# Earlier output products and cheaper pair products in a two-layer hybrid encoder

## The reference

```python
def even_mixer(...):            # S 256, 8 heads of 128, chunks along the sequence
    qkv = silu(centred_dwconv(p[..., :c1], conv_qkv))
    o = gated_delta_rule(q, k, v, g0, beta0) + flip(gated_delta_rule(flip(q), ...))
    o = o * rsqrt(mean(o * o, -1) + RMS_EPS) * out_gain
    y_dn = o * silu(gate)
    y_sc = b_gate * centred_dwconv(c_gate * u_in, conv_sc)
    return concatenate([y_dn, y_sc]) @ w_out          # 1024 + 1024 rows of w_out

def odd_mixer(...):             # RWKV: 8 heads of 64
    y = scan_forward + scan_backward
    yn = (y - mean(y)) * rsqrt(var(y) + RW_GN_EPS) * ln_w + ln_b   # per head
    y_d = (yn + bonus_0 + bonus_1) * gate
    return concatenate([y_c, y_d]) @ w_out            # y_c: attention, 512; y_d: 512
```

## Time and profile before

| | us |
|---|---|
| median of 3 runs | 3043.23 (3040.58 to 3050.79) |
| profiled execution, its own time | 3038.12 |
| its span, first to last instruction | 3036.0 |
| PE busy in the span | 2929.5 |
| even scan's four groups, from 378 | to 545 |
| first product of ev_out | 574.01 |
| odd scan's four groups, from 1896 | to 2126 |
| first product of od_out | 2143.79 |

### The profile page before, as it was taken

How to read it: one execution, slowest core, us unless ns; L and a number is a source line. 1 busy time by engine, 2 the same in 40 slices (tenths; PEclk the granted TensorE clock), 3 DMA queues, 4 the chain that set the end, 5 groups by cost and what they waited for, 6 DMA issues and landing times.

```text
span 3036.0 us, 45974 instructions
## 1 busy us (share of the span) xinstructions
PE 2929.5 (96%) x19074; PEld 2682.3 (88%) x19074; DVE 1569.0 (52%) x1923; ACT 1271.0 (42%) x1564; POOL 186.2 (6%) x169
## 2 busy tenths in 40 slices
PE   8999999899999999999999997999999999999999
PEld 7999989788998989899898896888888989898897
DVE  4555456565544454544545466543655444544544
ACT  4543322364544534444444444122455434444443
POOL 0000055100000000000000001432000000000000
PEclk9999999999999999999999999888999999999999
DMA  6454300344455555555445550001344555545554
GB/s 255 167 193 181 139 1 1 120 172 153 167 184 191 183 194 188 187 193 181 166 167 180 201 194 18 1 1 56 111 167 139 188 187 182 192 182 194 181 185 149
DMA packets 67918, 462.31 MB, mean 152 GB/s; under 512 B 7007, under 2 KB 10079, under 8 KB 12940
## 3 DMA queue, kind: packets, MB, share of 16 engines
q1 hardware_dynamic: 63680, 449.95, 41.6%
q10 hardware_dynamic: 3500, 5.21, 0.5%
q0 software_dynamic: 544, 4.19, 0.4%
HBM read 457.21 MB, written 5.27 MB: 152 GB/s over the span
## 4 chain that ended last, share of the span: by engine, by line
PE 90%; DVE 6%; ACT 2%; DMA 1%; issue 1%; POOL 0%; SPq 0%; DVEq 0%; ACTq 0%; POOLq 0%
PE bank L406 13%; PE bank L407 13%; PE bank L408 13%; PE bank L381 12%; PE bank L382 12%; PE bank L383 12%; PE bank L1028 3%; PE bank L1012 2%; PE bank L2008 1%; PE bank L1225 1%; PE bank L507 1%; DVE hT_lo L520 1%; DVE split_lo L332 0%; DMA par<-in_small 0%; DMA hwork<-bias_rows 0%
## 5 line engine op out<-in xcount | busy, mean ns | idle before, releaser
L332 DVE TENSOR_TENSOR split_lo<-raw,split_hi 128x1024 fp32r<-128x1024 f32 x840 | 1026.6, 1225 | 1089.8 <-ACT split_hi L325 1088.9
L325 ACT ACTIVATE split_hi<-raw 128x1024 fp32r<-128x1024 f32 x840 | 889.2, 1061 | 1289.3 <-PE bank L408 677.1
L406 PE MATMUL bank<-hT_hi,split_hi 128*128 128x256 f32 x3376 | 957.0, 283 | 10.3 <-issue 4.5
L407 PE MATMUL bank<-hT_lo,split_hi 128*128 128x256 f32 x3376 | 956.1, 283 | 0.0
L408 PE MATMUL bank<-hT_hi,split_lo 128*128 128x256 f32 x3376 | 956.0, 283 | 0.0
L406 PEld LDWEIGHTS bank<-hT_hi,split_hi 128*128 128x128 f32 x3376 | 648.7, 192 | 8.3 <-DVE split_lo L332 3.6
L407 PEld LDWEIGHTS bank<-hT_lo,split_hi 128*128 128x128 f32 x3376 | 648.7, 192 | 5.1 <-issue 4.8
L408 PEld LDWEIGHTS bank<-hT_hi,split_lo 128*128 128x128 f32 x3376 | 648.8, 192 | 0.0
L381 PE MATMUL bank<-split_hi,u_hi 128*128 128x512 f32 x1152 | 449.4, 390 | 0.0
L382 PE MATMUL bank<-split_lo,u_hi 128*128 128x512 f32 x1152 | 448.3, 389 | 0.0
L383 PE MATMUL bank<-split_hi,u_lo 128*128 128x512 f32 x1152 | 448.3, 389 | 0.0
(11 more groups left out here) (393 smaller groups left out, 2356.7 us busy)
## 6 DMA issues: line engine op xcount, KB each, us to landing
raw<-in_stream SPq DMA_DIRECT2D x420, 1024.0 KB, 4.8
work<-in_mem POOLq DMA_DIRECT2D x2, 2048.0 KB, 9.2
bias_rows<-bias_line SPq DMA_DIRECT2D x1, 3072.0 KB, 15.0
hwork<-bias_rows ACTq DMA_DIRECT2D x2, 1536.0 KB, 9.6
x<-in_x SPq DMA_DIRECT2D x1, 2048.0 KB, 9.4
out<-x SPq DMA_DIRECT2D x4, 512.0 KB, 5.0
const<-in_masks SPq DMA_DIRECT2D x1, 1665.5 KB, 12.9
work<-in_wide ACTq DMA_DIRECT2D x1, 1280.0 KB, 5.8
```

The source lines that it names most:

```text
L325: nc.scalar.activation(split_hi[:, u % SPLIT], raw[:, b % RAW, (u % 2) * UNIT:(u % 2 + 1) * UNIT], ACT.Copy).then_inc(s_hi, 1)
L332: nc.vector.tensor_tensor(split_lo[:, u % SPLIT], raw[:, b % RAW, (u % 2) * UNIT:(u % 2 + 1) * UNIT], f32(split_hi[:, u % SPLIT]), SUB).th ...
L406: nc.tensor.matmul(out, lhsT=w_hi[:, cols], rhs=hT_hi[:, k, :], start=k == 0, stop=False)
L407: nc.tensor.matmul(out, lhsT=w_hi[:, cols], rhs=hT_lo[:, k, :], start=False, stop=False)
```

## The change

Five edits; its lines stand up to 54 lower than the same ones before.

1. `ev_out` takes the convolution half first: its weight rows are stored in that order, k tiles 8 to 15 of hT are read before 0 to 7, hT of the convolution half is written earlier and in four pieces, and PE's 16 transpositions stand behind units 2 and 3 of chunk 0. The dummy products are gone. ACT and DVE split two more units before their waits for the transpositions.
2. The RWKV norm is by group: statistics of each group right behind its output copy; scaling of groups 0 to 2 in one pass, of group 3 in another. POOL prepares gate times ln_w, and (bonus + ln_b) times gate, in four passes of 128 x 1024 in groups 0 and 1. `od_out` starts with the attention half, and the transpositions of groups 2 and 3 stand behind its unit 1.
3. `pe_delta_pre` computes key and query products for direction 0 only; direction 1 reads them from banks 2 and 3.
4. The last group's output goes to bank 2 instead of 0 in both layers.
5. `pe_rwkv_pairs` goes by tile, then by matrix, with the two heads (row halves) innermost; groups 1 to 3 have four dummy products ahead of the wait of direction 0.

```diff
-            pe_keep_busy(bank[1], 11)
-            for b in range(4):
-                pe.wait_ge(s_y, b // 2 + 1)
...
-            pe_out_cross(pe, 0, "ev_out", KD, lambda k: pe.wait_ge(s_yT, min(k // 2 + 2, 5)))
+            def turn_heads(u):
+                if u not in (2, 3):
+                    return
+                pe.wait_ge(s_y, u - 1)
+                for b in range(2 * u - 4, 2 * u - 2):
...
+            pe_out_cross(pe, 0, "ev_out", KD, lambda k, t: hT_tile((k + 8) % KD, t),
+                         lambda k: pe.wait_ge(s_yT, k // 2 + 1), turn_heads)
...
+OUT_BANK = (0, 0, 0, 2)
-                    for bk, lhsT, rhs in ((b[0], g_col, const_of("causal", 2 * d + 1)), (b[1], b_col, ident),
-                                          (b[2], dn_kT[:, h, tile], dn_kT[:, h, tile]),
-                                          (b[3], dn_kT[:, h, tile], dn_qT[:, h, tile])):
+                    products = [(b[0], g_col, const_of("causal", 2 * d + 1)), (b[1], b_col, ident)]
+                    if d == 0:
+                        products += [(bank[2], dn_kT[:, h, tile], dn_kT[:, h, tile]),
+                                     (bank[3], dn_kT[:, h, tile], dn_qT[:, h, tile])]
...
             act_delta_tail(act, DN_GROUPS - 1, range(3))
+            act.wait_ge(s_qtg, 2 * DN_GROUPS)
+            for b in range(4):
+                nc.scalar.activation(hT_hi[:, 8 + 2 * b:10 + 2 * b, :], yscT[:, 2 * b:2 * b + 2, :], ACT.Copy).then_inc(s_ysp, 1)
             act.wait_ge(s_oms, 1)
             nc.scalar.activation(o_sd, o_ms, ACT.Sqrt).then_inc(s_osd, 1)
+            hi_upto(act, starts["ev_out"][1] + AHEAD + 2)
...
             dve_delta_R(dve, DN_GROUPS - 1)
+            for b in range(4):
+                dve.wait_ge(s_ysp, b + 1)
+                nc.vector.tensor_tensor(hT_lo[:, 8 + 2 * b:10 + 2 * b, :], yscT[:, 2 * b:2 * b + 2, :],
+                                        f32(hT_hi[:, 8 + 2 * b:10 + 2 * b, :]), SUB).then_inc(s_yT, 1)
             dve_delta_out(dve, DN_GROUPS - 1)
...
-            pe_keep_busy(bank[3], 30)
-            pe.wait_ge(s_ry, 1)
...
+            turn_heads(0)
+            pe_out_cross(pe, 1, "od_out", 8, hT_tile, lambda k: pe.wait_ge(s_yT, 9 + k // 2),
+                         lambda u: turn_heads(1) if u == 1 else None)
...
+            if f and d == 0:
+                pe_keep_busy(bank[3], 4)
...
-            for i in range(2):
-                for t in range(NT):
-                    bk = pair_banks(f, d)[2 * i + t]
-                    rows = slice(64 * i, 64 * i + 64)
-                    for j, lhs in enumerate((btl[f % 2], ktl[f % 2])):
+            for t in range(NT):
+                for j, lhs in enumerate((btl[f % 2], ktl[f % 2])):
+                    for i in range(2):
+                        bk = pair_banks(f, d)[2 * i + t]
+                        rows = slice(64 * i, 64 * i + 64)
...
             dve_rwkv_state(dve, RW_F - 1)
+            dve_rwkv_norm(dve, 0, 3, 2)
+            for b in range(2):
+                dve.wait_ge(s_ysp, b + 9)
...
             dve_rwkv_out(dve, RW_F - 1)
-            dve.wait_ge(s_os, RW_F + 4)
...
+            dve_rwkv_norm(dve, 3, 1, 3)
...
+            dve.wait_ge(s_os, f + 5)
+            y = y_heads(Ytok, f, 1)
+            dve_step(nc.vector.reduce_sum(norm_of(gsum, f, 1), y, AX_X))
+            dve_step(nc.vector.tensor_scalar(norm_of(gmean, f, 1), norm_of(gsum, f, 1), 1.0 / RW_N, None, MULT))
+            dve_step(nc.vector.tensor_tensor(y, y, wide_of(gmean, f, 1), SUB))
+            dve_step(nc.vector.tensor_tensor(y_heads(y_sq, 0, 1), y, y, MULT))
+            dve_step(nc.vector.reduce_sum(norm_of(gvar, f, 1), y_heads(y_sq, 0, 1), AX_X))
+            nc.vector.tensor_scalar(norm_of(gms, f, 1), norm_of(gvar, f, 1), 1.0 / RW_N, GN_EPS, MULT, ADD).then_inc(s_oms, 1)
...
+        def dve_rwkv_norm(dve, f, n, root):
+            dve.wait_ge(s_osd, root)
+            dve.wait_ge(s_gnw, 1)
+            y, own = y_heads(Ytok, f, n), slice(f * P, (f + n) * P)
+            dve_step(nc.vector.reciprocal(norm_of(grs, f, n), norm_of(gsd, f, n)))
+            dve_step(nc.vector.tensor_tensor(y, y, wide_of(grs, f, n), MULT))
+            dve_step(nc.vector.tensor_tensor(Ytok[:, :, own], Ytok[:, :, own], gout[:, :, own], MULT))
+            nc.vector.tensor_tensor(Ytok[:, :, own], Ytok[:, :, own], y_add[:, :, own], ADD).then_inc(s_y, 1)
...
+                    if f < 2 and level in (2, 3):
+                        pool_norm_weights(pool, 2 * f + level - 2)
```

More of the change, by code:

```diff
@@ L275, in build @@
             sem(n) for n in ("s_rc", "s_rF", "s_rRA", "s_rbk", "s_rM", "s_rMAT", "s_rbt", "s_rBK", "s_rz1", "s_rz1s"))
-        s_gms, s_gsd, s_ry, s_ryt = (sem(n) for n in ("s_gms", "s_gsd", "s_ry", "s_ryt"))
+        s_gnw = sem("s_gnw")
         block = ctx.enter_context(nc.Block())
@@ L1265, in pe_delta_tail @@
                     for i in range(2):
-                        out = bank[0][:, (2 * t + i) * P:(2 * t + i + 1) * P]
+                        out = bank[OUT_BANK[hp]][:, (2 * t + i) * P:(2 * t + i + 1) * P]
                         qkt = QKT[hp % 2]
@@ L1501, in dve_even @@
                 nc.vector.tensor_tensor(y_tok[:, :, own, :], y_tok[:, :, own, :], g4, MULT).then_inc(s_y, 1)
-            dve.wait_ge(s_ysp, 1)
-            nc.vector.tensor_tensor(hT_lo[:, 8:16, :], yscT, f32(hT_hi[:, 8:16, :]), SUB).then_inc(s_yT, 1)
+            lo_upto(dve, starts["ev_out"][1] + AHEAD + 2)
             for b in range(4):
-                dve.wait_ge(s_ysp, b + 2)
+                dve.wait_ge(s_ysp, b + 5)
                 nc.vector.tensor_tensor(hT_lo[:, 2 * b:2 * b + 2, :], aux[b][:, :].rearrange("p (h s) -> p h s", s=S),
@@ L1964, in pe_rwkv, with turn_heads @@
                 pe_rwkv_tail(pe, RW_F - 1, step)
-            pe_keep_busy(bank[3], 30)
-            pe.wait_ge(s_ry, 1)
-            for b in range(2):
+            def turn_heads(b):
+                pe.wait_ge(s_y, b + 3)
                 for i in range(2):
@@ L2066, in pe_rwkv_tail @@
                             h = 2 * f + i
-                            out = bank[0][:, t * P + i * RW_N:t * P + (i + 1) * RW_N]
+                            out = bank[OUT_BANK[f]][:, t * P + i * RW_N:t * P + (i + 1) * RW_N]
                             nc.tensor.matmul(out, lhsT=mat[:, d, 2 * i + t, 3], rhs=rv[:, t, h * RW_N:(h + 1) * RW_N],
@@ L2100, in between @@
                         hi_upto(act, starts["od_out"][1] + AHEAD)
+                    if f + 1 == RW_F and level == 5:
+                        act.wait_ge(s_oms, RW_F)
+                        nc.scalar.activation(norm_of(gsd, 0, 3), norm_of(gms, 0, 3), ACT.Sqrt).then_inc(s_osd, 1)
                 act_inv(act, 4 + f, rw_inv[f % 2], between)
@@ L2242, in dve_rwkv_pairs @@
         def dve_rwkv_pairs(dve, f, d):
-            for m_ in range(4):
-                dve.wait_ge(s_rM, 8 * f + 4 * d + m_ + 1)
+            for n, m_ in enumerate((0, 2, 1, 3)):
+                dve.wait_ge(s_rM, 8 * f + 4 * d + n + 1)
                 i0 = C["causal"].start + 256 * d
@@ L2267, in pool_rwkv_pre, with pool_norm_weights @@
                 nc.gpsimd.tensor_tensor(ktl[f % 2][:, d], f_cols(kdT[:, d], f), Fx[:, d, :, 2, :], MULT).then_inc(s_rbk, 1)
+        def pool_norm_weights(pool, step):
+            row = lambda j: ln_wb[:, j].unsqueeze(1).broadcast_to([P, NT, RW_W])
+            if step == 0:
+                pool.wait_ge(s_bon, 1)
+                pool.wait_ge(s_rv, 2)
+                pool.wait_ge(s_rgs, 2)
+                pool.wait_ge(s_wide, 32)
+                pool_step(nc.gpsimd.tensor_tensor(y_add.rearrange("p t (h e) -> p (t h) e", e=RW_N),
+                                                  rv.rearrange("p t (h e) -> p (t h) e", e=RW_N),
+                                                  lanes(bon.rearrange("p t h -> p (t h)"), RW_N), MULT))
+            elif step == 1:
+                pool_step(nc.gpsimd.tensor_tensor(y_add, y_add, row(1), ADD))
+            elif step == 2:
+                pool_step(nc.gpsimd.tensor_tensor(y_add, y_add, gout, MULT))
+            else:
+                nc.gpsimd.tensor_tensor(gout, gout, row(0), MULT).then_inc(s_gnw, 1)
         def pool_odd(pool):
@@ L2416 @@
         "ev_sc": np.hstack([sc[:, p * 1024 + h * 512:p * 1024 + h * 512 + 512] for p, h in sc_order]),
-        "ev_out": a["ev_w_out"][0],
+        "ev_out": np.vstack([a["ev_w_out"][0][DN_W:], a["ev_w_out"][0][:DN_W]]),
         "od_q": a["od_w_in"][0][:, :DSA_H * P],
```

83 lines of the change are left out of this document (36 added, 47 removed).

## The result

| | before | after |
|---|---|---|
| median of the runs, us | 3041.9 (4 runs: 3024.6 to 3050.8) | 3001.1 (4 runs: 3000.0 to 3002.4) |
| profiled execution, own time | 3038.12 | 3000.68 |
| its span | 3036.0 | 2998.9 |
| even scan's groups end, first product of ev_out | 562.91, 574.01 | 559.5, 559.50 |
| second pair call of group 3 | 2062.03 | 2032.69 |

The change is faster: ratio 0.9873, 95% interval 0.9829 to 0.9917. The two profiled executions stand 37.4 us apart where 50.4 were forecast; 3001 lies in the range, 8 us over the forecast of 2993.

The account below looks back on a forecast made before the run. TensorE, busy 96% of the span, was taken as the bound: its work, idle time and clock. Terms 5.4 + 9.3 + 20 + 1.3 + 15.1 - 0.7 = 50.4 us off the median 3043.23 gave 2993 us, range 2982 to 3011.

Parts of the forecast that it names:

- shared products, groups 1 to 3: Even scan: direction 1 issues 16 of 32 records at each group's start, 1.8 us less each, 5.4 us in all.
- ev_out: Even output product: convolution half starts behind the tail, 11.1 us of waiting less 1.8 for transpositions, 9.3 us gained.
- group 0's pairs: Odd scan, group 0: two shorter pair calls at half clock, partly covered by VectorE's masks, 1.3 us gained.
- pairs, groups 1 to 3: Odd scan: dummy products hold full clock and alternating halves shorten calls, 7.4 us a group less 2, 20 us gained.
- added VectorE and POOL work: Odd scan: new statistics operations and POOL passes cost 0.7 us, with bounds of 0 and 6.
- od_out: Odd output product: the 17.7 us between scan and first product shrink, 15.1 us gained.
- the second wait at 1.5 us: Odd scan, ahead of the second pair call: 1.5 us idle may lower the clock again, priced at -2 us.
- A clock that is not yet up behind the tail 0.5: Start of the odd output product: low clock behind the scan's tail costs 0.5 us of the gain.
- Half clock all the same at the pairs: Rival, odd scan: clock falls despite dummy products, pairs bring 7.5 instead of 20 us, time 3005; chance 0.20.
- Starved products: Rival, both output products: units 4 and up wait for split parts or hT, 3 us each, time 2999; chance 0.10.
- Halves that don't overlap: Rival, pair calls: row halves overlap no more than before, time 3000; chance 0.07.
- A slow odd scan: Rival: late VectorE work ahead of level 4 keeps the odd scan's clock low, 3077 at mean clock 0.65; chance 0.03.

Follow-up runs that it names:

- filled tails: Changed kernel with one or two dummy products ahead of each last-group tail step in both scans, two behind inverse levels 4 and 5; 2979.9 us, ratio 0.9811.
- shared_only: Kernel before with the shared key and query products alone; 3032.4 us, ratio 0.9978.
- after_again: Changed kernel, unchanged, profiled and timed again; 2995.2 us, ratio 0.9881.
- pairs_only: Kernel before with only the alternating row halves and the four dummy products at the pair calls; 3016.2 us, ratio 0.9931.
- even_out_only: Kernel before with only the edit of the even output product and its output bank 2; 3017.9 us, ratio 0.9944.
- odd_out_only: Kernel before with only the edit of the odd norm and output product and output bank 2; 3019.6 us, ratio 0.9938.

## Why the prediction was right, and where its terms were off

The working was made against one execution, so it is set beside the two profiled ones: 50.4 forecast, 37.1 measured by their spans. Gains in us. In the last column a pair of times is before and after, and a figure with a minus sign is how much earlier the changed kernel is at that place.

| term | forecast | measured | place of the reading |
|---|---|---|---|
| shared products, groups 1 to 3 | 5.4 | 3.4 | tail's end 562.91, 559.5 |
| ev_out | 9.3 | 9.3 | second chunk 12.7 earlier, less 3.4 |
| between, unchanged stages | 0 | -5.9 | -12.7 at ev_out, -6.8 at 1891 |
| group 0's pairs | 1.3 | 0.7 | first call of group 1, 1933.06, 1925.56 |
| pairs, groups 1 to 3 | 20 | 21.8 | -7.5, and -29.3 at 2062.03 |
| added VectorE and POOL work | -0.7 | 0 | in the line above |
| od_out | 15.1 | 11.8 | -29.3, and -41.1 behind its first chunk |
| last MLP | 0 | -4.0 | -41.1, and -37.1 at the end |

So 13.3 us of the 50.4 are missing: 9.9 in stages that no edit touches, 5.3 in two terms that were too large, 0.6 in group 0, less 2.5 where the terms were too small. That the forecast is only 8 us off has a part of luck in it: it was taken from the median of three runs, 3043.23, where the profiled execution had 3038.12.

- **Right in mechanism and size:** the even output product; the pair stretch (11.1 us from the first call's start to the second's end forecast, 11.05 measured; full overlap of the row halves). By this kernel's rows the measured call of 2.00 us against one of 2.94 is 8 slots for 12. The estimate from the Trainium skill's figure (TensorE: Matmul & The Clock Gate, Part 3, Measured speedup vs the span model), which is for four row tiles and not for two halves, was 2.6 us: the trace shows 2.00, and the reading of the earlier trace rows was the better guide.
- **Right in size by luck of the base:** "Gain 7.4 a group, 22 for three" was read off an execution in which all three groups had fallen, and the measured 21.8 is counted from the same one. Over six profiles of that pair code 10 of 18 fell, so on average a group has 1.9 us from the halves and some 3 from the clock: an estimate of about 15 us for three groups, not 20. The same holds for the base itself: the 49 timed executions of before lie between 3021 and 3051 with a mean of 3035, 8 under the median of three from which the 50.4 were taken. Both errors are the same error, one draw read as the kernel.
- **Wrong as a certainty:** "it fell right behind the 2.25 us wait" and the second wait at 1.5 us ("I take that in less than one group of the three"). A fall follows this wait in 10 of 18 groups, and in none of the 15 in which dummy products leave 0.5 us of it; behind the second call's wait of 1.27 us it fell in none of those 15 either. With alternating halves a fall costs 1.6 us instead of 5 to 6.
- **Mis-sized: the odd output product.** The gap went from 17.68 to 1.70 us, as forecast ("within 2 us"). "A clock that is not yet up behind the tail 0.5" measured 3.7: od_out's first chunk ran 44.15 - 41.1 = 3.05 us longer, of which 0.5 are the transpositions and 2.5 the clock, and 1.2 us more went from the second pair call to the tail's end (65.25 us for 64.08), at half clock. The 30 dummy products that were taken out had done their work: with them the clock was back at 1.00 before the first weight product. With filled tails od_out starts 7.2 us earlier (2092.44 for 2099.64), and its first chunk takes 2.6 less.
- **Mis-sized: the shared products.** The boundaries gave 1.6 and 3.4 us after one and two of them, on the way to 5.4; then the clock stood at 0.79 in the last tail (window 541.0 to 559.5). *shared_only* has the same fall, with nothing else changed, and the gain of 3.5 to 3.9 us over twelve profiles says that this is no draw: the 5.4 had no term for the clock in the last tail. Why it falls there for longer with this edit stays open.
- **Not in the sum:** clock falls in stages that no edit touches, and the last MLP's loop. They cost 9.9 us between the two profiled executions (5.9 and 4.0). The loop's part came again in *after_again* (7.1 us of idle time). The other is partly a draw: from the second chunk of ev_out to the first pair call pass 1300.6 us in the first profile of before and 1305.0 and 1301.0 in the next two, 1306.5 and 1303.2 in the two of the changed kernel. The intervals of the single edits hold this too: the gains of *pairs_only*, *even_out_only*, *shared_only* and *odd_out_only* add up to 2.1%, 64 us, where the full change has 1.3%, 39 us. Each of the four has none of the 3.7 to 4.5 us of idle time that before has there (15 to 18 of the 25 us), and the full change has 6.9; the rest lies within the intervals.
- **The rivals.** Half clock all the same at the pairs: no, 15 of 15 held. Starved products: no gap in either chunk 0. Halves that don't overlap: no. A slow odd scan: VectorE's level 4 L1070 lost its 2.31 us of room (2067.65, right behind L2277) but was not late: it starts 1.10 us behind its L1028 run, as before. The statistics products did not meet POOL either: L2274 and L2275 took 0.42 to 0.43 us in all four groups, so of the bounds of 0 and 6 us for that it was 0.

## What to carry to other kernels

A stretch at half clock in one profile is a draw: before a price is put on it, profile the same code two or three times, and price it by how often it falls. Dummy products that fit into a wait cost nothing that these traces show (four in a wait of 2.25 us, one or two in waits of about 0.5 to 1.3 us), and the clock held behind the four in 15 of 15 groups and through both filled odd tails. They are no guarantee: the 11 of the kernel before stand ahead of further waits, and in 5 of 8 profiles the clock was down again when ev_out began. When such products are removed ahead of a long run of full-rate work, look at whether the clock is up when that run begins. When a change of a few tenths of a per cent is to be read, compare the stages that no edit touches first: what they gain or lose is not the edit's.

## What the runs showed of the hardware that was not expected

Products of 64 rows in alternating row halves run in pairs without loss: 16 records in 2.00 us for 2.94. The clock behind an unchanged wait of 2.25 us fell in 10 of 18 groups, and at the unchanged start of ev_out in 5 of 8 profiles. The idle time in a loop of weight products, 0, 0.4, 3.7 to 4.7 or 7 us in three turns, keeps with the kernel and not with the execution; its cause is open. The longest is followed by a stretch at 0.50.
